# A two-block attention and delta-rule model on one core: the first two inverse levels as 32 by 32 blocks in array quarters, squares in one activation, steps in a new order

## What is computed

```python
kb = k * beta[..., None]
lower = jnp.where(strict, jnp.einsum('bhnid,bhnjd->bhnij', kb, k) * decay, 0.0)
tmat = jnp.eye(CHUNK) + lower
u = triangular_solve(tmat, v * beta[..., None], lower=True, unit_diagonal=True)
w = triangular_solve(tmat, kb * jnp.exp(gc)[..., None], lower=True, unit_diagonal=True)
...
def l2_normalize(x):
    return x * lax.rsqrt(jnp.sum(x * x, axis=-1, keepdims=True) + NORM_EPS)
```

## Time and profile before

| what | value |
|---|---|
| median of three runs | 1058.83 us (1057.62 to 1060.48) |
| span of the profiled execution | 1056.6 us, 2.2 us under the median of the runs |
| instructions in the profile | 18561 |

### The profile page before, as it was taken

The page is one execution under the profiler, slowest core; times in us unless marked ns, Lnnn a source line. Parts: engine busy times, 40 slices in busy tenths (PEclk is TensorE's granted clock), DMA queues, the critical chain, the costliest instruction groups (busy, mean ns, idle before and its releaser), DMA issues.

```text
span 1056.6 us, 18561 instructions
## 1 busy us (share of the span) xinstructions
PE 1025.6 (97%) x7112; PEld 886.4 (84%) x7112; DVE 599.0 (57%) x1181; ACT 577.4 (55%) x968; POOL 712.2 (67%) x550
## 2 busy tenths in 40 slices
PE   8999999999999999999999998999999989999986
PEld 8988998888877988899888887788888768888875
DVE  4774366786565557246584563517446560646564
ACT  4754347656644574336656744445576534567652
POOL 4786537872648787556766645897366978744794
PEclk9999999999999999999999999999999999999999
DMA  8664434653425555435444332665233546423451
GB/s 294 192 179 122 139 101 131 173 156 107 134 100 153 180 165 157 140 84 157 141 139 141 115 125 87 209 191 158 81 113 120 186 140 216 133 91 108 140 183 57
DMA packets 80584, 151.59 MB, mean 143 GB/s; under 512 B 6448, under 2 KB 12400, under 8 KB 80496
## 3 DMA queue, kind: packets, MB, share of 16 engines
q1 hardware_dynamic: 80496, 150.41, 46.9%
HBM read 149.34 MB, written 1.05 MB: 142 GB/s over the span
## 4 chain that ended last, share of the span: by engine, by line
PE 88%; DVE 4%; ACT 3%; POOL 3%; issue 2%; DMA 0%; POOLq 0%; SPq 0%; DVEq 0%; ACTq 0%
PE bulk L941 53%; PE bulk L926 12%; PE chain L962 5%; PE chain L970 4%; PE chain L1039 4%; PE chain L1307 1%; PE bulk L934 1%; PE chain L1288 1%; ACT arena L1347 1%; PE chain L1163 1%; PE chain L1179 1%; POOL w_lo L868 1%; DVE arena L1846 1%; PE chain L1030 1%; POOL w_lo L866 1%
## 5 line engine op out<-in xcount | busy, mean ns | idle before, releaser
L866 POOL TENSOR_TENSOR w_lo<-raw,w_hi 128x512 fp32r<-128x512 f32 (+3 forms) x259 | 340.7, 1316 | 292.4 <-ACT w_hi L1347 291.8
L868 POOL TENSOR_TENSOR w_lo<-raw,w_hi 128x512 fp32r<-128x512 f32 (+3 forms) x277 | 375.6, 1357 | 31.8 <-ACT w_hi L1347 31.8
L1347 ACT ACTIVATE w_hi<-raw 128x1024 fp32r<-128x1024 f32 (+4 forms) x277 | 277.3, 1019 | 210.1 <-PE bulk L941 163.4
L941 PE MATMUL bulk<-w_hi,hT_hi 128*128 128x512 f32 (+1 forms) x756 | 306.0, 405 | 0.8 <-ACT arena L1347 0.5
L941 PE MATMUL bulk<-w_hi,hT_lo 128*128 128x512 f32 (+1 forms) x756 | 294.4, 389 | 0.0
L941 PE MATMUL bulk<-w_lo,hT_hi 128*128 128x512 f32 (+1 forms) x756 | 204.2, 389 | 1.9 <-POOL w_lo L868 1.9
L941 PEld LDWEIGHTS bulk<-w_hi,hT_hi 128*128 128x128 f32 x756 | 142.4, 188 | 33.5 <-issue 1.9
L941 PEld LDWEIGHTS bulk<-w_lo,hT_hi 128*128 128x128 f32 x756 | 141.7, 188 | 32.7 <-POOL w_lo L868 3.4
L941 PEld LDWEIGHTS bulk<-w_hi,hT_lo 128*128 128x128 f32 x756 | 142.5, 188 | 26.8 <-issue 1.0
L926 PE MATMUL bulk<-hT_hi,w_hi 128*128 128x256 f32 x384 | 96.3, 289 | 0.0
L926 PE MATMUL bulk<-hT_lo,w_hi 128*128 128x256 f32 x384 | 94.0, 282 | 0.0
(11 more groups left out here) (262 smaller groups left out, 1393.4 us busy)
## 6 DMA issues: line engine op xcount, KB each, us to landing
raw<-in_w_in_dram SPq DMA_DIRECT2D x194, 512.0 KB, 3.6
raw<-in_w_out_dram SPq DMA_DIRECT2D x32, 512.0 KB, 3.7
raw<-in_w_branch_dram SPq DMA_DIRECT2D x16, 512.0 KB, 3.7
raw<-in_w_mem_kv_dram SPq DMA_DIRECT2D x8, 512.0 KB, 3.4
raw<-in_w_merge_up_dram SPq DMA_DIRECT2D x16, 256.0 KB, 2.9
raw<-in_w_in_dram SPq DMA_DIRECT2D x8, 420.0 KB, 3.4
gain<-in_ln_rows_dram SPq DMA_DIRECT2D x4, 512.0 KB, 5.3
gain<-in_gains_dram SPq DMA_DIRECT2D x3, 512.0 KB, 6.1
```

Source lines behind the costliest of these rows:

```text
L866: pool.tensor_tensor(lo_of(p, u)[:, 0:at], raw_of(p, u)[:, 0:at], hi_of(p, u)[:, 0:at].bitcast(F32), ALU.subtract).then_inc(first_part, 1)
L868: pool.tensor_tensor(lo_of(p, u)[:, at:n], raw_of(p, u)[:, at:n], hi_of(p, u)[:, at:n].bitcast(F32), ALU.subtract).then_inc(p.done("split" ...
L941: m = pe.matmul(dst, a, part[:, k, :], start=(first and not low and k == 0 and i == 0), stop=(last and low and k == nk - 1))
L1347: return act.activation(dst, src, func, **more)
```

## The change

It has three parts. First, `x1` and the levels 0 and 1 of the inverse work on the four 32 by 32 diagonal blocks of each matrix, each in its own quarter of the array's rows and columns (`quad_blocks`). What were 16 matmuls of 64 by 64 in `half_blocks` are 32 of 32 by 32. The tiles become half as wide on DVE and ACT too: `xq` and `xtq` (the inverse in both orientations) and `yq`. A new ACT step `x2` after level 0 spreads the quarters into the halves, where level 2 goes on as before, and at level 1 DVE subtracts into the halves in two operations for each orientation (`apart`). Second, `stat` is one activation that squares 1024 columns in place in PSUM, and a DVE reduction that sums. Third, `ORDER` is another string; apart from the four `x2` it holds the same steps.

```diff
+def level_mask(n):
+
+    return (K_LEVEL + n * QUAD, QUAD) if n < 2 else (K_LEVEL + 2 * QUAD, HALF)
...
+        if n == 0:
+            out.append(("x2", g))
         if n == 0:
             out.append(("vT", g))
...
 ORDER = (
-    "aaaaasammssvamsmssaamaaasaacsccasscccssammcmmsmaacssmmaacssccsmmmamaaaasasmdabsmaaabssmmcsmaammassdbm"
...
+    "aaaaasamsmsvasaassmmsmaasaasmacsccsmammcccamcsasmscamasamccsmsmcamsaamsasdambsacmsmabsaammsamamsdbam"
...
-    "baT": "vector", "memT": "vector", "cwT": "vector", "hT": "vector", "gc": "vector", "stat": "scalar", "dec": "vector", "avT": "scalar",
+    "baT": "vector", "memT": "vector", "cwT": "vector", "hT": "vector", "gc": "vector", "stat": "vector", "dec": "vector", "avT": "scalar",
...
+        quads = [slice(q * QUAD, (q + 1) * QUAD) for q in range(4)]
+        xq, xtq, yq = xx8[:, :, HALF:HALF + QUAD], xx8[:, :, HALF + QUAD:P], yy8[:, :, 0:QUAD]
...
+                def quad_blocks(c, pair, col=0):
+
+                    for j in range(R * 4):
+                        for at in quads:
+                            a, b = pair(j, at)
+                            m = pe.matmul(c[at, col + j * QUAD:col + (j + 1) * QUAD], a, b, start=(j == 0), stop=(j == R * 4 - 1),
+                                          skip_group_check=True)
+                    return m
...
-                    half_blocks(c, lambda j, at: (xth[at, j, :], ident[at, at])).then_inc(p.done("x1"), 1)
+                    quad_blocks(c, lambda j, at: (xtq[at, j, :], ident[at, at])).then_inc(p.done("x1"), 1)
...
-                    if n < len(LEVELS) - 1:
+                    if n < 2:
+                        quad_blocks(c, lambda j, at: (lt8[at, j, at], xq[at, j, :])).then_inc(p.done("invY"), 1)
+                    elif n < len(LEVELS) - 1:
...
+                    if n < 2:
+                        quad_blocks(c, lambda j, at: (xtq[at, j, :], yq[at, j, :]))
+                        quad_blocks(c, lambda j, at: (yq[at, j, :], xtq[at, j, :]), 512).then_inc(p.done("invZ"), 1)
+                    elif n < len(LEVELS) - 1:
...
-                    for r in range(R):
-                        for j in range(4):
-                            x = c[:, (4 * r + j) * P:(4 * r + j + 1) * P]
-                            ins = A(x, x, ACT.Square, accum_out=s2[:, w, r, j:j + 1])
-                    ins.then_inc(p.done("stat"), 1)
+                    A(c[:, :], c[:, :], ACT.Square).then_inc(p.done("stat"), 1)
...
+                def x2(g):
+
+                    act.wait_ge(*p.after("vector", "invX", g, 0))
+                    for to, of in ((xh, xq), (xth, xtq)):
+                        for n in range(2):
+                            ins = A(to[:, :, n * QUAD:(n + 1) * QUAD], of, ACT.Copy, scale=cst[:, K_PART + n:K_PART + n + 1])
+                    ins.then_inc(p.done("x2"), 1)
...
+                    v.tensor_reduce(sums, half("stat", w, g)[:, :].rearrange("p (a n) -> p a n", n=P), AX, ALU.add).then_inc(p.own, 1)
+                    v.wait_ge(*p.last())
                     TS(sums, sums, EPS, None, ALU.add).then_inc(p.done("stat"), 1)
...
-                    for r in range(R):
-                        for j in range(4):
-                            ins = TT(xth[:, 4 * r + j, :].rearrange("p (b i) -> p b i", i=BLK),
-                                     over(inv[:, 4 * r + j, :], HALF // BLK), blocks, ALU.mult)
+                    ins = TT(xtq.rearrange("p m (b i) -> p m b i", i=BLK),
+                             inv[:, :, :].unsqueeze(2).broadcast_to([P, R * 4, QUAD // BLK, BLK]),
+                             blocks.unsqueeze(1).broadcast_to([P, R * 4, QUAD // BLK, BLK]), ALU.mult)
...
+                def apart(to, c):
+
+                    for k in range(2):
+                        x = to[:, :, k * QUAD:(k + 1) * QUAD]
+                        ins = STT(x, c, cst[:, K_PART + 2 + k:K_PART + 3 + k], x, ALU.mult, ALU.add)
+                    return ins
```

More of the change, by code:

```diff
@@ L332 @@
+    "mysvvvmssmsmvemmeesvmvmmvmsvemmmaeesasmmaamsbmmssammmsdmmsmmsmssssmmmddasmaassmmbsmsbmmabbdsasmdmsam"
+    "sasbbbaammdsaabbdbsmbbmsaavabmbssbasbmdmabmsbbyddssmbsbmmabmmassyyddmbamyasssbsydmssdvsbdsyyvmvyvmss"
+    "dmmvmmsdvmsvvsyvmmsmmmvsvvmmsvvssyvvsvvesmeemvmmvmmvmmveemem"
 )
@@ L1518, in x1 @@
                     act.wait_ge(*p.after("tensor", "x1", g))
-                    A(xh, heads(half("x1", g)[:, 0:R * 4 * HALF], R * 4), ACT.Copy).then_inc(p.done("x1"), 1)
+                    A(xq, heads(half("x1", g)[:, 0:R * 4 * QUAD], R * 4), ACT.Copy).then_inc(p.done("x1"), 1)
+                def x2(g):
[4 more added lines that the diff above has]
+                    ins.then_inc(p.done("x2"), 1)
                 def half(*key):
@@ L1993, in invY @@
                     v.wait_ge(*p.after("tensor", "invY", g, n))
+                    if n < 2:
+                        at, w = level_mask(n)
+                        TT(yq, heads(half("invY", g, n)[:, 0:R * 4 * w], R * 4), over(cst[:, at:at + w], R * 4),
+                           ALU.mult).then_inc(p.done("invY"), 1)
+                        v.wait_ge(*p.here("invY"))
+                        return None
                     c, up = heads(half("invY", g, n)[:, 0:R * 4 * HALF], R * 4), halves[1]
@@ L1997, in invY @@
                     else:
-                        m = cst[:, K_LEVEL + n * HALF:K_LEVEL + (n + 1) * HALF]
-                        TT(yh, c, over(m, R * 4), ALU.mult).then_inc(p.done("invY"), 1)
+                        at, w = level_mask(n)
+                        TT(yh, c, over(cst[:, at:at + w], R * 4), ALU.mult).then_inc(p.done("invY"), 1)
                     v.wait_ge(*p.here("invY"))
+                def apart(to, c):
[3 more added lines that the diff above has]
+                    return ins
                 def invZ(g, n):
                     v.wait_ge(*p.after("tensor", "invZ", g, n))
+                    if n < 2:
+                        c = heads(half("invZ", g, n)[:, 0:R * 4 * QUAD], R * 4)
+                        if n == 0:
+                            TT(xq, xq, c, ALU.subtract).then_inc(p.done("invZ"), 1)
+                        else:
+                            v.wait_ge(*p.after("scalar", "x2", g))
+                            apart(xh, c).then_inc(p.done("invZ"), 1)
+                        v.wait_ge(*p.here("invZ"))
+                        return None
                     c, (low, up) = heads(half("invZ", g, n)[:, 0:R * 4 * HALF], R * 4), halves
@@ L2012, in invX @@
                 def invX(g, n):
+                    if n < 2:
+                        c = heads(half("invZ", g, n)[:, 512:512 + R * 4 * QUAD], R * 4)
+                        if n == 0:
+                            TT(xtq, xtq, c, ALU.subtract).then_inc(p.done("invX"), 1)
+                        else:
+                            apart(xth, c).then_inc(p.done("invX"), 1)
+                        v.wait_ge(*p.here("invX"))
+                        return None
                     c = heads(half("invZ", g, n)[:, 512:512 + R * 4 * HALF], R * 4)
```

46 lines of the change are left out of this document (22 added, 24 removed).

## The result

The changed kernel takes 1080.34 us (median of four runs, 1075.84 to 1083.02) against 1059.65 for the kernel before in the same rounds. The ratio on record is 1.0172, with a 95% interval of 1.0131 to 1.0214; the two medians alone give 1.0195, which lies within it. The change makes the kernel slower by 18 us (by the ratio) to 21 us (by the medians), where 10 us less were forecast. The profiled execution has a span of 1081.2 us against 1056.6.

A forecast was written before the change was run, and what follows sets the result against it. PE, busy for 97% of the span, was taken to bound the kernel. Span 1056.6 − 26.0 + 14.3 (inverse matmuls) + 1.0 + 0.6 (order) = 1046.5, plus 2.2 to the median: 1048.7 us, range 1040 to 1066.

The forecast's parts named there:

- The quarters: Inverse's matmuls in 32 by 32 blocks, four tiles side by side: .008 us a record, gain of 11.7 us; chance .56.
- The floor for every record: Rival: PE issues the 1792 records at a set distance whatever their width; at .029 a record 1086.4 us; chance .14.
- two tiles at a time: Rival: weight loads or PSUM writes pair off two by two, .016 a record, 1063.1 us; chance .14.
- The matmuls of the inverse: `x1`, `invY` and `invZ` on PE: 26.0 us removed, 14.3 us added.
- Three places, and one pair, can change a wait: New order: PE's total stays, only these spots change waits; sum +1.6 us, between −4 and +7.
- Place 2: At `mT 1`: the .64 wait for DVE goes, PE waits 1.65 before `o0.2`; net +1.0 us.
- place 3: Between the layers: PE asks for `hT`'s first half two pieces earlier; taken as 0, between −1.6 and +4 us.
- place 1: `invY` to `invZ`, DVE's mask between: shortfalls of .1 to .2 us, some four of them, +0.6 us.
- the pair `gT 1`: Second block: its 2.7 us wait in layer 1 may go, one like it come in layer 0; taken as 0, ±2.7.
- It costs nothing: DVE's and ACT's work in the inverse, `x2` included, lies beside PE's bulk, where both have room: 0 us.
- The squares: ACT's 64 squares with readouts, 29.6 us, become eight, 8.1, plus DVE reductions, 9.8; hidden under PE: 0, −1 to +1.
- The third, the order taking it back: Rival: quarters gain 11.7 us, but places 1 to 3 cost +7 and late weight splits 3; 1057.1 us, chance .06.

The follow-up runs named there:

- quads_tuned: The kernel before with the quarters alone, on the old order and squares, `x2` moved in three of its four places: .9914, 1054.09 us.
- order_only: The kernel before with the new `ORDER` alone, without its four `x2`, old halves and squares: 1.0181, 1081.03 us.
- quads_only: The kernel before with the quarters alone, on the old order and squares, `x2` put just ahead of `vT`: 1.0095, 1070.62 us.
- stat_only: The kernel before with the new squares alone (one activation and a DVE reduction): 1.0048, 1066.89 us.

## Why the prediction was wrong

- **The quarters: right.** Measured without the waits: 64 records in .75 us, and PE busy for 10.6 us less in `quads_tuned`, where 11.7 were forecast. The floor for every record, and two tiles at a time, did not come; the 60 cycles for each matmul that the Trainium skill gives ("TensorEngine Tiling (Array Packing)", section "Instruction Overhead") are not paid between quarters.
- **"The matmuls of the inverse" as the whole price: wrong.** The term left out that twice as many instructions also have to be brought to PE. In the changed kernel it measured 10.1 us in five waits, nearly all of the gain, and some lower clock behind three of them.
- **"Three places, and one pair, can change a wait", with all other moves of the order at nothing and a sum of +1.6, between −4 and +7: wrong, and this step carries the sign.** `order_only` is 19 us slower, without quarters and without the new squares. What was priced came out nearly as priced. Place 2 in layer 0 has waits of 1.3 and 1.6 us where .64 stood (+2.3, forecast +1.0; the 1.6 is the 1.65 of the prediction, but the .64 doubled where it was to go), place 3 has 1.4 where .23, .38 and 1.39 stood (−.6, forecast 0), place 1 has none (forecast +.6), and the pair `gT 1` moved its wait (+.2, forecast 0). Together this is +1.9. Places 2 and 3 after:

```profile
320.68 1.94 PE L974 MATMUL chain<-cst,arena 128*128 128x128 f32 x16 [1.32 <-DVE arena L2284]
324.25 0.50 PE L953 MATMUL bulk<-w_hi,hT_hi 128*128 128x512 f32 x1 [1.63 <-DVE hT_lo L2289]
...
342.25 1.07 PE L974 MATMUL chain<-cst,arena 128*128 128x128 f32 x8 [1.38 <-DVE arena L1783]
```

  The loss lies in what was put at nothing. The largest part that has a name is place 2 once more, in layer 1: 2.85 us of wait became 6.80. DVE's time for the mix was taken from the trace of before (2.19), in which POOL happened to rest. The effect was in the earlier trace rows, a step of .16 that took 1.20 beside POOL, and was used at place 3 only, for a gain. At place 2 the question was the same: which splits now run there. The rest is spread over many waits of under 2 us each; those for L1851 (2.5 us in two) and L1984 (1.9 in two) are new and were not followed up.
- **"It costs nothing" for the other engines: wrong as an argument, though not what failed here.** The share of busy time was true, but an engine's queue has an order. This showed on the old order only: in the changed kernel neither `x2` nor the addition makes PE wait. In `quads_only`, `x2` in one bad place made PE wait 3.7 us, more than the 2 that were given as the bound, and in three places 12 in all (3.7, 4.7 and 2.1, 1.8). The squares were put at 0, between −1 and +1, and cost 5 in `stat_only`, through one small addition that was there before. The sum for ACT's squares was wrong as well: it added readouts that overlap the squares, so ACT is busy for 10 us less and not for 21.
- **The rivals.** The third, the order taking it back, named the side that lost but gave it .06 and 1057; it capped each place at its price without POOL. A chain of small DVE steps has no such cap.

Of the 24.9 us in which PE stands still more than before, 10.1 are the waits for instructions and nearly all of the remaining 14.8 waits for DVE (about 13) and ACT (about 2); the quarters' 10.6 us and the lower clock's estimated 8 nearly cancel in PE's busy time. What part of the lower clock each wait brings was not told apart. How the new order would do with the splits, `x2` and the instruction blocks all put right was not tried; the best version that was run is `quads_tuned`.

## What to carry to other kernels

When a step is moved, ask not only what it waits for but what will run beside it on POOL: a DVE operation between two on-chip tiles has one duration alone and another beside POOL, and the trace of before shows only one of them at that place. When matmuls are made smaller and more, count instructions per microsecond as well as time per matmul, and keep long matmuls between the short ones. A new step on a free engine still needs a place in that engine's queue where nothing urgent stands behind it, and moving three such steps was worth 1.8% here (from 1.0095 to .9914).

## What the hardware showed that was not expected

- PE stops at the end of a block of 256 instructions when the next one has not arrived: fifteen of fifteen waits at the same count modulo 256, of .6 to 3.6 us, and each ends 1.3 to 1.6 us after a load of 16 KB has landed. How long a block lasts does not decide alone: four of the changed kernel's waits came behind blocks of 1.9 to 2.2 us and one behind 4.1, while blocks of 2.5 and 3.1 us passed without, as their loads had landed earlier. What sets the start of a load was not found.
- Four tiles of 32 by 32 start a 32-bit record each .0084 us (128 records in 1.29 us and 64 in .75, so .54 / 64). The step from halves to quarters brought a factor of 3.4 for each record (.029 to .0084), not far from the four of half the width and twice the tiles.
- An addition to 128 by 8 numbers on DVE, .17 us at its shortest, took 3.46 us beside three POOL subtractions; DVE did not get in between them.
